# One block of a two-part transformer on a Trainium2 core: the second batch of the modulation's products formed partly on GpSimd

## What is computed

```python
c_act = jax.nn.silu(c)                                   # (1, 1024)
mod = c_act @ w_ada[l] + b_ada[l]                        # (1, 6 * 1024)
sh1, sc1, gt1, sh2, sc2, gt2 = jnp.split(mod, 6, axis=-1)
h = rms_norm(x, g_norm1[l]) * (1.0 + sc1) + sh1
proj = h @ w_in[l]
...
x = x + gt1 * (merged @ w_o[l])
h2 = rms_norm(x, g_norm2[l]) * (1.0 + sc2) + sh2
...
x = x + gt2 * ((jax.nn.silu(a) * up) @ w_ffn_out[l])
```

## Time and profile before

| | us |
|---|---|
| median of 3 runs | 2263.01 (2259.01 to 2263.64) |
| the profiled execution's own time | 2256.2 |
| its span in the profile | 2254.4 |
| TensorE busy (matmuls) | 2141.8 |
| VectorE busy | 1330.2 |
| ScalarE busy | 1137.2 |
| GpSimd busy | 61.4 |

### The profile page before, as it was taken

One profiled execution on the slowest core, in us unless ns is written; L12 is line 12 of the kernel. 1 busy time (PEld: TensorE's weight loads), 2 busy tenths in 40 slices (PEclk: granted clock), 3 DMA queues, 4 the chain that ended last, 5 costly groups with the idle time before them and its releaser, 6 DMA issues. The chain is left out here.

```text
span 2254.4 us, 40901 instructions
## 1 busy us (share of the span) xinstructions
PE 2141.8 (95%) x15620; PEld 1874.1 (83%) x15620; DVE 1330.2 (59%) x1845; ACT 1137.2 (50%) x1673; POOL 61.4 (3%) x74
## 2 busy tenths in 40 slices
PE   6999889999999999989999999999999997999998
PEld 5787778887888988888998887887997897998887
DVE  3446375556556985565655555555896564756555
ACT  3453644445445555654445445444556563535444
POOL 0000000000000010000000000000002000000000
PEclk8999999999999999999999999999999999999999
DMA  9663245554553443421455554554444321355553
GB/s 398 235 240 111 75 157 187 186 186 170 188 187 145 184 157 127 166 79 58 151 186 194 186 186 170 189 187 167 155 180 150 140 104 41 131 187 186 187 186 121
DMA packets 53328, 373.24 MB, mean 166 GB/s; under 512 B 6304, under 2 KB 6304, under 8 KB 9280
## 3 DMA queue, kind: packets, MB, share of 16 engines
q1 hardware_dynamic: 47664, 342.00, 41.9%
q0 software_dynamic: 5520, 29.23, 3.6%
HBM read 370.10 MB, written 1.11 MB: 165 GB/s over the span
## 5 line engine op out<-in xcount | busy, mean ns | idle before, releaser
L1419 ACT ACTIVATE HI<-ring 128x1024 fp32r<-128x1024 f32 x606 | 625.1, 1054 | 762.8 <-PE banks L536 397.6
L1962 DVE TENSOR_TENSOR LO<-ring,HI 128x1024 fp32r<-128x1024 f32 x318 | 389.1, 1226 | 369.2 <-ACT HI L1419 368.9
L1968 DVE TENSOR_TENSOR LO<-ring,HI 128x2048 fp32r<-128x2048 f32 x139 | 318.5, 2291 | 255.1 <-ACT HI L1419 249.7
L500 PE MATMUL banks<-UH,HI 128*128 128x256 f32 x1392 | 406.4, 292 | 5.3 <-DVE LO L1968 5.3
L501 PE MATMUL banks<-UL,HI 128*128 128x256 f32 x1392 | 396.2, 285 | 0.0
L502 PE MATMUL banks<-UH,LO 128*128 128x256 f32 x1392 | 396.1, 285 | 0.0
L534 PE MATMUL banks<-HI,UH 128*128 128x512 f32 x896 | 349.4, 390 | 7.1 <-DVE LO L1968 4.9
L536 PE MATMUL banks<-HI,UL 128*128 128x512 f32 x896 | 348.7, 389 | 0.0
L535 PE MATMUL banks<-LO,UH 128*128 128x512 f32 x896 | 348.7, 389 | 0.0
L500 PEld LDWEIGHTS banks<-UH,HI 128*128 128x128 f32 x1392 | 269.3, 193 | 22.6 <-issue 15.9
L501 PEld LDWEIGHTS banks<-UL,HI 128*128 128x128 f32 x1392 | 269.5, 194 | 1.4 <-issue 1.2
(11 more groups left out here) (326 smaller groups left out, 3089.9 us busy)
## 6 DMA issues: line engine op xcount, KB each, us to landing
ring<-in_w_stream SPq DMA_DIRECT2D x315, 1024.0 KB, 4.8
ARENA<-in_ada_stream POOLq DMA_DIRECT2D x16, 1024.0 KB, 5.1
ARENA<-in_ada_stream SPq DMA_DIRECT2D x8, 1024.0 KB, 14.8
GRMS<-cum_rows POOLq DMA_DIRECT2D x16, 256.0 KB, 3.5
ARENA<-in_na_bias POOLq DMA_DIRECT2D x2, 1024.0 KB, 13.2
RMS<-cum_rows POOLq DMA_DIRECT2D x8, 256.0 KB, 3.4
RSTD<-cum_rows POOLq DMA_DIRECT2D x8, 256.0 KB, 3.7
ARENA<-in_ropes POOLq DMA_DIRECT2D x1, 1088.0 KB, 18.7
```

The source lines that it names most:

```text
L500: nc.tensor.matmul(out, lh, rh, start=start, stop=False, **kw)
L1419: nc.scalar.activation(HI[:, q % PARTS, at], ring[:, q % RING, at], ACT.Copy).then_inc(hi_ready, 1)
L1962: nc.vector.tensor_tensor(LO[:, q % PARTS, at], ring[:, q % RING, at], HI[:, q % PARTS, at].bitcast(F32), ALU.subtract).then_inc(lo_ready, 1)
L1968: nc.vector.tensor_tensor(LO[:, q % PARTS, :], ring[:, q % RING, :], HI[:, q % PARTS, :].bitcast(F32), ALU.subtract).then_inc(lo_ready, 2)
```

## The change

The second batch no longer goes through `ada_rows`. For every panel GpSimd multiplies the eight k tiles in place by their columns of silu(c) (one instruction of 128 x 2048, the columns broadcast), adds the upper half of the tiles to the lower (128 x 1024, then 128 x 512), and writes the last sum (128 x 256) into one of four accumulators `ADA_ACC`, which lie in `RMS`, `RSTD` and `GRMS`. Every step waits on the semaphore `ada_acc` for the step before. Then it issues the load of the panel after next. After four panels TensorE makes `ada_sums(m)`: four matmuls with a one-hot stationary operand, which sum each accumulator over the partitions into its panel's row. GpSimd writes the accumulators again only after that. The four calls stand behind `head_spread(1)`, behind n = 2 and n = 5, and behind n = 7. The first batch is made as before; its eight loads share three semaphores in place of four.

```diff
+ADA1_GROUP = (0, 0, 0, 0, 1, 1, 2, 2)
...
+        ADA_ACC = [RMS[:, 0:S], RMS[:, S:2 * S], RSTD[:, S:2 * S]]
...
+        ADA_ACC.append(GRMS[:, 3, :])
...
-            for n in range(ADA_FIRST + 2, ADA_PANELS):
-                pool.wait_ge(ada_rows_done, n - 1)
-                pool.dma_start(ADA2[:, n % 2, :], ada_stream[n]).then_inc(ada2_loaded[n % 2], 16)
+            pool.wait_ge(c_ready, 1)
+            for n in range(ADA_FIRST, ADA_PANELS):
+                i = n - ADA_FIRST
+                src, acc = tiles(ADA2[:, n % 2, :], KT), ADA_ACC[n % 4]
+                pool.wait_ge(ada2_loaded[n % 2], 16 * (i // 2 + 1))
+                if i >= 4:
+                    pool.wait_ge(ada_rows_done, ADA_FIRST + i // 4 * 4)
+                nc.gpsimd.tensor_tensor(src, src, CPAD[:, :, 31:32].to_broadcast([P, KT, S]), ALU.mult).then_inc(ada_acc, 1)
+                for step, half in enumerate((4, 2)):
+                    pool.wait_ge(ada_acc, 4 * i + step + 1)
+                    nc.gpsimd.tensor_tensor(src[:, 0:half, :], src[:, 0:half, :], src[:, half:2 * half, :], ALU.add).then_inc(ada_acc, 1)
+                pool.wait_ge(ada_acc, 4 * i + 3)
+                nc.gpsimd.tensor_tensor(acc, src[:, 0, :], src[:, 1, :], ALU.add).then_inc(ada_acc, 1)
+                if n + 2 < ADA_PANELS:
+                    pool.wait_ge(ada_acc, 4 * i + 4)
+                    pool.dma_start(ADA2[:, n % 2, :], ada_stream[n + 2]).then_inc(ada2_loaded[n % 2], 16)
...
+            def ada_sums(m):
+
+                pe.wait_ge(ada_acc, 16 * (m + 1))
+                if m == 0:
+                    pe.wait_ge(ada_taken, 1)
+                for g in range(4):
+                    n = ADA_FIRST + 4 * m + g
+                    mm = nc.tensor.matmul(bank[6][32 * g:32 * g + 32, 0:S], ONEHOT[:, 31 - n:63 - n], ADA_ACC[g], start=(m == 0),
+                                          stop=(m == 3))
+                mm.then_inc(ada_rows_done, 4)
...
-            ada_rows(ADA_FIRST)
             for q in range(1, 5):
                 b1_panel(q)
                 head_sums(q - 1)
-                ada_rows(ADA_FIRST + q)
             b1_panel(5)
             head_spread(0)
             head_spread(1)
-            ada_rows(ADA_FIRST + 5)
+            ada_sums(0)
...
-                if n < 6:
-                    ada_rows(ADA_FIRST + 6 + n)
-                else:
-                    ada_rows(2 * n + 8)
-                    ada_rows(2 * n + 9)
+                if n in (2, 5):
+                    ada_sums((n + 1) // 3)
                 if 1 <= n <= 6:
                     head_sums(NA_PAIRS + n - 1)
+            ada_sums(3)
             b1_half(14, 0)
             ada_columns(1)
```

More of the change, by code:

```diff
@@ L281, in build_program @@
         uh_ready, ul_ready = sem("uh_ready"), sem("ul_ready")
-        ada1_loaded = [sem(f"ada1_loaded{i}") for i in range(ADA_FIRST // 2)]
+        ada1_loaded = [sem(f"ada1_loaded{i}") for i in range(3)]
         ada2_loaded = [sem(f"ada2_loaded{i}") for i in range(2)]
@@ L285, in build_program @@
             sem("ada_rows_done"), sem("ada_taken"), sem("ada_done"), sem("ada_copied"))
+        ada_acc = sem("ada_acc")
         gu_done, hid_product, hid_turned, hidh_ready = (
@@ L396, in _ @@
             for i in range(ADA_FIRST):
-                sp.dma_start(ADA1[:, i, :], ada_stream[i]).then_inc(ada1_loaded[i // 2], 16)
+                sp.dma_start(ADA1[:, i, :], ada_stream[i]).then_inc(ada1_loaded[ADA1_GROUP[i]], 16)
             def load(q, slot):
@@ L685, in ada_rows @@
             def ada_rows(n):
-                if n < ADA_FIRST:
-                    pe.wait_ge(ada1_loaded[n // 2], 32)
-                    src = tiles(ADA1[:, n, :], KT)
-                else:
[L691 to L694, removed]
+                pe.wait_ge(ada1_loaded[ADA1_GROUP[n]], 16 * ADA1_GROUP.count(ADA1_GROUP[n]))
+                src = tiles(ADA1[:, n, :], KT)
                 for k in range(KT):
@@ L697, in ada_rows @@
                     mm = nc.tensor.matmul(bank[6][group, 0:S], CPAD[:, k, 31 - n:63 - n], src[:, k, :],
-                                          start=(n in (0, ADA_FIRST) and k < 4),
-                                          stop=(n in (ADA_FIRST - 1, ADA_PANELS - 1) and k >= 4))
+                                          start=(n == 0 and k < 4), stop=(n == ADA_FIRST - 1 and k >= 4))
                 mm.then_inc(ada_rows_done, 1)
+            def ada_sums(m):
[7 more added lines that the diff above has]
+                mm.then_inc(ada_rows_done, 4)
             def ada_columns(batch):
```

## The result

| | before | changed |
|---|---|---|
| median of 5 runs | 2260.98 us | 2319.43 us |
| lowest, highest | 2259.01, 2263.64 | 2313.55, 2322.14 |
| profiled execution | 2256.2 us | 2317.56 us |
| its span | 2254.4 us | 2315.7 us |

The ratio of the runs is 1.0261, with an interval of 1.0247 to 1.0275: slower by 58 us. Forecast were 2320, and 2288 to 2350.

What follows compares the result with a forecast made beforehand. TensorE bound the stretch before; GpSimd's chain would after: start 40 + 147.4 panels + 32 shared access + 2.8 turns = 222.2 us, a 57.4 us delay, with 2.9 for the clock +60.3, so 2320 us, range 2288 to 2350.

Steps and rivals of the forecast that it cites:

- Rival (b): Same GpSimd chain, but VectorE's splits hardly cost it anything: end at 190 us, 2281 to 2291 us; chance 0.12.
- rival (c): GpSimd's chain keeps up with TensorE and the 16.1 us are gained: 2240 to 2247 us; chance 0.05.
- rival (d): Longer handovers (+15), multiply (+3), late start (+2), full port price (+4.5), second slow clock spell: up to 2350 us; chance 0.08.
- the handovers: GpSimd's semaphore waits for its own previous step: 0.1 us each, four times a panel; bounds 0 and 0.33.
- What goes: On TensorE, 16 panels' products (18.5 us) leave and four ada_sums (2.4 us) come: 16.1 us gained if nothing waited.
- A panel of GpSimd: GpSimd's arithmetic 8.35 us, issue 0.53 and handovers 0.4: 9.28 us a panel, 147.4 us for 16 less two issues.
- The start: GpSimd's chain starts at 40 us, taken between 38.5 and 41.9, after panel 8 lands.
- The shared access: GpSimd stands still during VectorE's splits and UL subtractions in the stretch: 32 us, bounds 0 and 36.5.
- The price for VectorE and TensorE: Splits up to 4.5 us late against TensorE's 3.8 us slack per panel: about 1 us where they bite.
- The turns and the end: GpSimd waits three times for ada_sums, 2.8 us; its chain ends at 222.2 us, the last ada_sums at 222.8.
- The clock: After its wait of some 15 us TensorE runs at half speed for 5.7 us, costing 2.9 us.
- What follows: Everything behind the last ada_sums starts 57.4 us later, otherwise unchanged; nothing takes the delay back, +60.3 us in all.

Runs made afterwards that it cites:

- the first experiment: Changed kernel with VectorE's splits of panels 2 to 15 cut to 64 of 2048 columns: 2299.18 us, ratio 1.0169.
- the control: Kernel before the change with VectorE's splits of panels 2 to 15 cut to 64 of 2048 columns: 2257.01 us, ratio 0.9991.

## Why the prediction was right

The forecast of 2320 us met 2319.4, and for its main reason: GpSimd's chain with the shared access is the bound (small splits gave 20 us, leaving out the multiply 44). Rival (b) fell with the chain's end at 212.9 us and the first experiment's 25 us, rival (c) with the waits of L719 in the changed kernel. Of rival (d)'s terms the handovers, the multiply, the start and the shared access all measured less; more slow clock spells there were, at each of the four ada_sums, but three of them lie ahead of a further wait. That it came within 1 us is luck, owed to errors that cancel. By its steps:

- **What goes.** 16.1 us was too much. The run without the batch gave 3.3 us less than its busy time says: a group's busy time is what an engine spends, not what it would finish earlier, and a part of these products stood in TensorE's waits. The ada_sums took 1.08 us each at a granted clock of 0.50, not 0.6. The 16.1 us are not in the sum, since the chain is the bound; the 0.6 is, in the turns, and there GpSimd waited 0.73, 0.44 and 0.44 us for the 0.93 forecast.
- **A panel of GpSimd.** 9.28 us forecast, 9.20 measured, out of other parts: the multiply 3.63, not 4.35, since the broadcast operand made 2048 columns cheaper than two full ones (4.53 in the earlier trace rows); the two larger adds 3.69 (3.77 with the handover between them), with 3.45 expected, because the add of 512 columns took 1.26 us where I had used the 1.05 of a multiply with a broadcast operand; 128x256 took 0.73 and not 0.55; the issue 0.59 for 0.53; the handovers three times 0.08 and once 0.30 for four times 0.1.
- **The start.** 39.03 us, with 40 forecast. The row shows that GpSimd waited for the landing until then, so readying its arithmetic cost nothing that could be seen.
- **The shared access.** 27 us, with 32 taken and 0 to 36.5 as bounds: the chain's 173.9 us less 145.1 for undisturbed panels (14 of 9.20 and the last two, which issue nothing, of 8.15) and 1.6 for the three turns. The splits' size is 25 of it. The Trainium skill (SBUF — State Buffer, "SBUF: two separate sides") states an exclusive lock, by which the prediction set the price at the full 36.5. The trace agrees with the lock; the full price wasn't reached in this kernel.
- **The price for VectorE and TensorE.** Here a step failed: "about 1 us where they bite". A chain that nobody waits for cost 17.2 us. I had looked only at the splits under way, and these TensorE's slack of 3.8 us per panel does cover, in the main. I had left out the start, where the UL subtractions are held, and the first softmax, where TensorE waits for VectorE already in the kernel before: 12.0 us up to the mark. In the changed kernel the chain's end sets when TensorE may go on, so such delays ahead of it can hide in TensorE's waits, which is why the sum didn't suffer; no run measures them there.
- **The turns and the end.** The chain ended at 212.9 us, not 222.2: 5 us from the port, the rest from start, panel and turns. The waits were 0, 9.1, 15.0 and 21.8 us for the forecast 8, 12, 18 and 18, in all 45.8 for 56.
- **The clock.** Resuming at 213.4 us TensorE ran at half speed for 3.0 us, where I had used 5.7:

```profile
213.40:216.40 3.00, 3.00 (x19) 2.44 (x12) 2.08 (x2) 0.00 (x0) 0.00 (x0) 0.50 0.00 0
216.40:225.00 8.60, 8.60 (x75) 8.13 (x74) 3.06 (x5) 2.49 (x3) 0.00 (x0) 1.00 0.01 2
```

- **What follows.** "All after it as before, shifted" was right up to 1050 us and wrong after it. The shift was 49.2 us and not 60.3, and some 9 us (12.1 between the two profiles) came later at a lower granted clock. This cancels the shortfall. The other runs' profiles grow behind the stretch by between 0.9 and 12.9 us against the same profile of before, each read from one execution. The three that leave at least 12 of the batch's 16 panels to TensorE (the control, four panels on GpSimd, products in the waits) grow by 0.9, 1.5 and 2.8 us, all others by 6.6 or more, those where nobody waits for GpSimd included. So the long waits alone can't be the cause; what is, and how much differs from run to run, is open.

By the medians of the runs the steps are: 10 us gained by sparing TensorE, 17 lost by the chain beside its work, and 53 (2319.4 - 2266.5) when TensorE has to wait for the chain and four more panels are in it, all with what comes behind the mark (at the marks the three are 9.9, 12.0 and 47.1). They sum to 60 and not 58 because the runs of before beside them had medians 1.5 us apart.

## What to carry to other kernels

An idle engine's busy share tells nothing of whether a serial chain fits: multiply the chain out per item (here 9.2 us by 16) and set it against the stretch before its result is due. If GpSimd is to compute beside a stage that VectorE feeds with operations of two SBUF inputs, charge both sides: GpSimd's own time grows, and TensorE's stage too, here by 12 us even when nobody waits for GpSimd (the whole kernel by 17). Look for that cost where TensorE already waits for VectorE, and not where it has slack. And if work looks cheap to move off the bounding engine, first try to put it where that engine waits: this gave 2.7 us in the stretch, 5.6 by the medians, without using another engine.

## What the runs showed of the hardware

- GpSimd's 128x2048 multiply with a broadcast operand took 3.63 us, while the subtraction with two full operands took 4.53. An add of 1024 and one of 512 columns took 3.77 together with the handover between them, one of 256 0.73 us. The Trainium skill (GPSIMD Engine Reference, "Elementwise — side-by-side cycle accounting") gives about 2.6 cycles per element for two inputs. An estimate from it, at 1.2 GHz, is 4.4 us for 2048 columns, which fits the full operands and not the broadcast one.
- GpSimd's fills of 2048, 1024, 512 and 256 columns took 1.82, 0.95, 0.53 and 0.31 us. They left VectorE's two-input splits at 2.29 us, but held a 128x2 operation with one input for 1.19 us in the mean, 0.17 otherwise. In the changed kernel it took up to 3.99 us:

```profile
99.00 3.99 DVE L2174 TENSOR_SCALAR ARENA<-ARENA 128x2 f32<-128x2 f32 x1
```

  The Trainium skill (SBUF — State Buffer, "SBUF: two separate sides") makes this very distinction: a VectorE operation with two SBUF inputs is excluded only by a GpSimd operation that reads SBUF, one in a 2-port mode by any GpSimd operation. The runs agree on the first part; whether the 128x2 operation runs in such a mode no run here shows. I had not looked for the one-input operations in my sum.
- GpSimd's wait for its own previous instruction costs 0.08 us between two arithmetic ones, and 0.30 before a transfer's issue.
